# A three-layer transformer kernel in which the rounded right operands of three stages start further on within a 2,048-byte row than their weights

## The chip, the cores and the metric

The kernel runs on one core of a Trainium2 chip, on 512 positions of width 1,024. The core has five engines with queues of their own: TensorE (PE; its weight loads are shown apart, as PEld), VectorE (DVE), ScalarE (ACT), GpSimd (POOL) and SyncE (SP, which issues the transfers from memory here). They share an on-chip memory (SBUF) of 128 partitions. An address in it is a byte within a partition; a word is 4 bytes. The metric is the device time in microseconds (us) of one execution, as the median of several.

## The reference, cut to what matters

Three layers, each a mixer and a feed-forward part, run one behind the other. All their projections are products of the activations with weight matrices, in fp32:

```python
def first_block(x, ...):          # two layers: neighborhood attention, differential attention
    for i in range(DEPTH):
        h = rms_norm(x, g[0])
        m = neighborhood_attention(h, ...) if i % 2 == 0 else diff_attention(h, ...)
        x = x + rms_norm(m, g[1])
        f = conv_glu_ffn(rms_norm(x, g[2]), ffn_w_in[i], ..., ffn_w_out[i])
        ...
# third layer (the hybrid one): three mixers on one input projection, then a feed-forward part
#   p = rms(x) @ w_in                      (1024 x P_IN)
#   mix = [rwkv7(p), mla(p), gated_deltanet(p)];  x = x + mix @ w_out
#   x = x + square(relu(rms(x) @ w_ff1)) @ w_ff2     (1024 x 4096, 4096 x 1024)
```

## The kernel before

Activations lie transposed: 128 channels on the partitions, 512 positions along each. A projection's weights come from memory in chunks of 128 partitions x 1,024 words (8 blocks of 128x128), through a ring of four buffers (`ring`), asked for by SP.

Every fp32 product is made of three products of rounded numbers (type float32r). `Splitter` holds them: ACT rounds a weight chunk into `w_hi` (`round_chunk`, L278), DVE writes what was lost into `w_lo` (`split_chunk`, L284), and the right operands are split in the same way into `r_hi` and `r_lo`. `multiply` (L293 to L301) then issues for each block

```python
pe.matmul(psum, hi, self.hi(rhs_slot), start=start, stop=False)     # L299: w_hi with r_hi
pe.matmul(psum, hi, self.lo(rhs_slot), start=False, stop=False)     # L300: w_hi with r_lo
return pe.matmul(psum, lo, self.hi(rhs_slot), start=False, stop=stop)   # L301: w_lo with r_hi
```

Each of the three loads a block of 128x128 weights and streams a right operand of 128x512 words through the array. PE fetches the weights of the following product while the current one streams. The profile names operands as out<-right operand,weights.

Four kinds of stages do this. Stage `l` holds both layers of the first block (tiles `l_w_hi`, `l_r_hi`, and the further slots `na_more_hi`, `na_more_lo`, `da_more_hi`, `da_more_lo`). The hybrid layer has `in2` (`mixer_inputs`; 27 chunks, tiles `in_...` in the profile), `mt` (`mixer_tail`; 8 chunks) and `ff` (`up_down`; 32 chunks up and 32 down). Between `in2` and `mt` lie two stages without a `Splitter`. The order of the work is written out by hand: each engine runs its own list and waits on semaphores. PE waits for a chunk's split (`chunk_split`), and ACT rounds the next chunk into a slot once PE is done with the one in it (`chunk_done`).

SBUF is given out in the order in which tiles are named, one behind the other, at multiples of 32 bytes. Let the place of a tile be its address modulo 2,048 bytes (512 words), and the distance of a right operand the words by which its place lies behind that of its weights. A slot of a right operand has 512 words, and a weight chunk 1,024, so a tile behind such tiles alone has distance 0. In `l`, `in2`, `mt` and `ff`, `w_hi`, `w_lo`, `r_hi` and `r_lo` follow one another with nothing between: `r_hi` and `r_lo` have distance 0. So do `da_more_hi` and `da_more_lo`. Only `na_more_hi` and `na_more_lo` don't: three small tiles of 16 words each (`na_nmax`, `na_tot`, `na_inv`) lie ahead of them, and both have distance 48. They hold the right operands of six of the eight blocks of each chunk of the neighborhood attention's projection; the first two blocks take theirs from `l_r_hi` and `l_r_lo`. A weight block lies at a multiple of 128 words in its chunk, so these distances differ by 128, 256 or 384 words from block to block, all else equal.

Of the kernel before, what the change touches and what calls it, by code (L numbers as in the profile page):

```python
# [18 lines left out]
F32R = mybir.dt.float32r  # L19
# [7 lines left out]
P = 128  # L27
S = 512
TT = S // P
D = 1024  # L30
DT = D // P
# [26 lines left out]
SLOTS = 4  # L58
# [112 lines left out]
class Program:  # L171


    def __init__(self, nc, ctx, dram):
        self.nc, self.dram = nc, dram
        self.sb = lambda name, shape, dt=F32: ctx.enter_context(nc.sbuf_tensor(name, shape, dt))
        with ExitStack() as under:
            self.qk_hi = under.enter_context(nc.sbuf_tensor("qk_hi", [P, 4, S], F32R))
        self.X = self.sb("X", [P, DT, S])
        self.H = self.sb("H", [P, DT, S])  # L180
        self.rstd = self.sb("rstd", [P, S])
        self.ring = self.sb("ring", [P, RING, BLK * P])
        self.par = self.sb("par", [P, N_PARAMS])
        self.const = self.sb("const", [P, N_CONSTS])
        self.ring_full = [ctx.enter_context(nc.semaphore(f"ring_full{i}")) for i in range(RING)]
        self.chunk_split = ctx.enter_context(nc.semaphore("chunk_split"))
        self.const_loaded = ctx.enter_context(nc.semaphore("const_loaded"))
        self.par_loaded = ctx.enter_context(nc.semaphore("par_loaded"))
        self.x_loaded = [ctx.enter_context(nc.semaphore(f"x_loaded{j}")) for j in range(DT)]
        self.chunk_done = ctx.enter_context(nc.semaphore("chunk_done"))  # L190
        self.g = 0
# [58 lines left out]
class Splitter:  # L250
# [2 lines left out]

    def __init__(self, k, st, rhs_tiles, rhs_slots=None, slots=SLOTS):
        self.k, self.g0, self.rhs_slots, self.slots = k, k.g, rhs_slots or rhs_tiles, slots
        self.w_hi = st.sb("w_hi", [P, slots, BLK * P], F32R)
        self.w_lo = st.sb("w_lo", [P, slots, BLK * P], F32R)
        self.r_hi = st.sb("r_hi", [P, rhs_slots or rhs_tiles, S], F32R)  # L260
        self.r_lo = st.sb("r_lo", [P, rhs_slots or rhs_tiles, S], F32R)
        self.more = []
        self.w_rounded, self.rhs_rounded, self.rhs_split = (
            st.sem(n) for n in ("w_rounded", "rhs_rounded", "rhs_split"))
# [292 lines left out]
def up_down(k, name, n_up, n_down, evacuation, mid, pre):  # L557


    with Stage(k, name) as st:  # L560
        sp_ = Splitter(k, st, DT, DT + 2)
        banks = st.ps("banks", [P, 8, S])
        front = Front(k, st, sp_, None, pre, banks[:, 6:8, :])
        bank_free, tile_done, added, stored = (st.sem(n) for n in ("bank_free", "tile_done", "added", "stored"))
# [1399 lines left out]
IN_SLOTS = 3  # L1964
# [8 lines left out]
def mixer_inputs(k, pi, kr, bi, ki, pc, rows2, cols):  # L1973
# [6 lines left out]
    order = in2_order()  # L1980
    shifted = [c for c in range(IN_T) if order[c] not in (MISC, G_GATE, G_GATE + 1, G_GATE + 2, M_Q, M_Q + 1, M_KV)]
    with Stage(k, "in2") as st:
        sp_ = Splitter(k, st, DT, slots=IN_SLOTS)
        acc = st.ps("acc", [P, 4, S])
        side = st.ps("side", [P, 4, S])
        bank_a, bank_b, bank_c, bank_d = (side[:, n, :] for n in range(4))
# [1102 lines left out]
OUT_SLOTS = 3  # L3089
# [3 lines left out]
def mixer_tail(k, pi, y, la):  # L3093
# [4 lines left out]


    with Stage(k, "mt") as st:  # L3100
        sp_ = Splitter(k, st, DT, slots=OUT_SLOTS)
        a = st.ps("a", [P, 5, S])
        ms = la.ms
        vt = st.sb("vt", [P, TT, 256])
# [478 lines left out]
def hybrid(k):  # L3583

    with ExitStack() as ctx:
        def sb(name, shape):
            return ctx.enter_context(k.nc.sbuf_tensor(name, shape, F32))

        pi = sb("pi", [P, IN_T, S])
        bi = sb("bi", [P, MIX_T, S])  # L3590
        kr = sb("kr", [P, MIX_T, TT, 2, P])
        ki = sb("ki", [P, MIX_T, S])
        v, gk, gv = pi[:, R_V:R_V + MIX_T, :], pi[:, G_K:G_K + MIX_T, :], pi[:, G_V:G_V + MIX_T, :]
        y = [v[:, i, :] for i in range(MIX_T)] + [gv[:, i, :] for i in range(MIX_T)]
        with ExitStack() as ctx2:
            def sb2(name, shape):
                return ctx2.enter_context(k.nc.sbuf_tensor(name, shape, F32))

            pc, el = sb2("pc", [P, MIX_T, NCH]), sb2("el", [P, MIX_T, NCH])
            rows2 = sb2("rows2", [P, S])  # L3600
            cols = sb2("cols", [P, 120])
            mixer_inputs(k, pi, kr, bi, ki, pc, rows2, cols)
            mt, n0 = sb2("mt", [P, 2 * MIX_T, NCH, CHUNK]), sb2("n0", [P, 2 * MIX_T, NCH, CHUNK])
            rows = [pi[:, R_WA, :], pi[:, R_G, :], rows2]
            chunk_operators(k, pi, bi, kr, ki, mt, n0, pc, el, rows, cols)
            la = Latent(pi, bi, ki, kr, ctx.enter_context(k.nc.psum_tensor("la_ms", [P, 3, S], F32)))
            recurrence(k, mt, n0, [bi[:, i, :] for i in range(MIX_T)] + [gk[:, i, :] for i in range(MIX_T)], (v, gv), pi, la)
        mixer_tail(k, pi, y, la)
    with ExitStack() as ctx:
        mid = ctx.enter_context(k.nc.sbuf_tensor("mid", [P, FF2_T, S], F32))  # L3610
        up_down(k, "ff", FF2_T, FF2_T, relu_squared(k, mid), mid, "ln_ffn")
# [121 lines left out]
```

## Time and profile before

| | us |
|---|---|
| median of 3 runs | 2222.01 |
| lowest, highest | 2221.18, 2223.2 |
| span of the profiled execution | 2221.5 |

The profiled execution's span is 0.5 us under the median. The trace has 14,078 products on PE and as many weight loads. A product's time in the trace (0.39 us for one of 128x512) runs from its start to the end of its results, and the next product starts long before that end. The pace of PE is therefore read from the distance between the starts of two products that follow one another, or from the number of products in a stretch, never from a sum of their times.

### The profile page before, as it was taken

Reading aid. Unit: us, or ns where it says so; the run is one execution under the profiler, and the core shown is the slowest. Engines: PE = TensorE matmul, PEld = TensorE weight load, DVE = VectorE, ACT = ScalarE, POOL = GpSimd, SP = SyncE. Lnnn points to the kernel's source line nnn. Section 1 sums busy time; section 2 is a strip of 40 time slices with the busy share of each in tenths; the row PEclk is TensorE's granted clock in tenths of the full one; section 3 lists DMA queues with packets and bytes.
Section 4 is the critical chain, followed back from the end, with each engine's and each line's share of the span. In section 5 each row is a group of like instructions: output and inputs, shape, how many; then the busy total and the mean of one; then the engine's idle time right before and its main releaser. Section 6 shows DMA issues by size and latency. Waiting matters only on the chain. (4 is left out here: it accounts for less than half of the span.)

```text
span 2221.5 us, 35739 instructions
## 1 busy us (share of the span) xinstructions
PE 2158.3 (97%) x14078; PEld 1723.8 (78%) x14078; DVE 1289.8 (58%) x1733; ACT 907.8 (41%) x1421; POOL 119.7 (5%) x96
## 2 busy tenths in 40 slices
PE   8999999999999999999999998999898899999999
PEld 6777788888877777778888876777787566888887
DVE  5564576663378877476665347686456566333333
ACT  4444532222365666642222244654322545323321
POOL 0000011110000000001110000000333000000000
PEclk9999999999999999999999999999999999999999
DMA  7332233333324221323333331322000112333321
GB/s 255 105 107 65 76 113 96 94 98 101 94 75 134 91 66 47 105 74 106 95 100 99 94 95 50 100 85 76 3 4 4 47 39 64 107 94 102 97 94 66
DMA packets 54087, 189.77 MB, mean 85 GB/s; under 512 B 5968, under 2 KB 6224, under 8 KB 53840
## 3 DMA queue, kind: packets, MB, share of 16 engines
q1 hardware_dynamic: 53680, 187.49, 27.3%
q8 instruction: 88, 1.44, 0.3%
q10 hardware_dynamic: 288, 0.59, 0.1%
q14 instruction: 31, 0.25, 0.0%
HBM read 184.91 MB, written 3.15 MB: 85 GB/s over the span
## 5 line engine op out<-in xcount | busy, mean ns | idle before, releaser
L299 PE MATMUL l_banks<-l_r_hi,l_w_hi 128*128 128x512 f32 x1440 | 574.3, 399 | 3.5 <-DVE l_r_lo L1796 2.3
L301 PE MATMUL l_banks<-l_r_hi,l_w_lo 128*128 128x512 f32 x1440 | 561.0, 390 | 0.0
L300 PE MATMUL l_banks<-l_r_lo,l_w_hi 128*128 128x512 f32 x1440 | 560.8, 389 | 0.0
L284 DVE TENSOR_TENSOR l_w_lo<-ring,l_w_hi 128x1024 fp32r<-128x1024 f32 x216 | 299.0, 1386 | 96.0 <-ACT l_w_hi L278 92.3
L278 ACT ACTIVATE l_w_hi<-ring 128x1024 fp32r<-128x1024 f32 x216 | 227.1, 1056 | 293.8 <-PE l_banks L301 288.9
L299 PEld LDWEIGHTS l_banks<-l_r_hi,l_w_hi 128*128 128x128 f32 x1440 | 270.3, 188 | 72.7 <-issue 8.2
L300 PEld LDWEIGHTS l_banks<-l_r_lo,l_w_hi 128*128 128x128 f32 x1440 | 270.5, 188 | 57.6 <-issue 4.3
L301 PEld LDWEIGHTS l_banks<-l_r_hi,l_w_lo 128*128 128x128 f32 x1440 | 270.3, 188 | 57.0
L299 PE MATMUL ff_banks<-ff_r_hi,ff_w_hi 128*128 128x512 f32 x512 | 200.0, 391 | 0.0
L301 PE MATMUL ff_banks<-ff_r_hi,ff_w_lo 128*128 128x512 f32 x512 | 199.2, 389 | 0.0
L300 PE MATMUL ff_banks<-ff_r_lo,ff_w_hi 128*128 128x512 f32 x512 | 199.2, 389 | 0.0
L735 POOL TENSOR_TENSOR tail_mid<-H 128x512 f32 x44 | 60.0, 1365 | 1145.8 <-ACT H L728 774.0
L284 DVE TENSOR_TENSOR ff_w_lo<-ring,ff_w_hi 128x1024 fp32r<-128x1024 f32 x64 | 78.3, 1225 | 61.6 <-ACT ff_w_hi L278 58.4
L299 PEld LDWEIGHTS ff_banks<-ff_r_hi,ff_w_hi 128*128 128x128 f32 x512 | 96.1, 188 | 20.5 <-issue 0.5
L300 PEld LDWEIGHTS ff_banks<-ff_r_lo,ff_w_hi 128*128 128x128 f32 x512 | 96.1, 188 | 20.2 <-issue 0.5
L301 PEld LDWEIGHTS ff_banks<-ff_r_hi,ff_w_lo 128*128 128x128 f32 x512 | 96.1, 188 | 20.1
L292 DVE TENSOR_TENSOR l_r_lo<-tail_mid,l_r_hi 128x512 fp32r<-128x512 f32 x44 | 30.5, 692 | 130.3 <-ACT l_r_hi L288 130.3
L299 PE MATMUL in_acc<-in_r_hi,in_w_hi 128*128 128x512 f32 x216 | 90.9, 421 | 0.0
L288 ACT ACTIVATE l_r_hi<-tail_mid 128x512 fp32r (+1 forms) x44 | 27.7, 630 | 153.1 <-PE l_banks L301 153.1
L301 PE MATMUL in_acc<-in_r_hi,in_w_lo 128*128 128x512 f32 x216 | 85.0, 393 | 0.0
L300 PE MATMUL in_acc<-in_r_lo,in_w_hi 128*128 128x512 f32 x216 | 84.7, 392 | 0.0
L292 DVE TENSOR_TENSOR ff_r_lo<-mid,ff_r_hi 128x512 fp32r<-128x512 f32 x32 | 22.2, 693 | 101.6 <-ACT ff_r_hi L288 101.6
(513 smaller groups left out, 3256.9 us busy)
## 6 DMA issues: line engine op xcount, KB each, us to landing
ring<-weights SPq DMA_DIRECT2D x315, 512.0 KB, 3.6
na_bias<-window_bias SPq DMA_DIRECT2D x16, 512.0 KB, 5.4
da_rel<-t_rel SPq DMA_DIRECT2D x8, 448.0 KB, 4.2
outT<-X SPq DMA_DIRECT2D x12, 256.0 KB, 2.1
X<-xT SPq DMA_DIRECT2D x8, 256.0 KB, 5.7
const<-consts SPq DMA_DIRECT2D x1, 1312.0 KB, 11.5
l_pt<-pT SPq DMA_DIRECT2D x2, 512.0 KB, 4.6
X<-outT SPq DMA_DIRECT2D x4, 256.0 KB, 3.2
```

Source lines behind the costliest of these rows:

```text
L278: act.activation(self.w_hi[:, c % self.slots, :], k.ring[:, g % RING, :], ACT.Copy).then_inc(self.w_rounded, 1)
L284: dve.tensor_tensor(self.w_lo[:, c % self.slots, :], k.ring[:, g % RING, :], self.w_hi[:, c % self.slots, :].bitcast(F32), ALU.subtract).t ...
L288: act.activation(self.hi(slot), src, ACT.Copy).then_inc(self.rhs_rounded, 1)
L292: dve.tensor_tensor(self.lo(slot), src, self.hi(slot).bitcast(F32), ALU.subtract).then_inc(self.rhs_split, 1)
L299: pe.matmul(psum, hi, self.hi(rhs_slot), start=start, stop=False)
L300: pe.matmul(psum, hi, self.lo(rhs_slot), start=False, stop=False)
L301: return pe.matmul(psum, lo, self.hi(rhs_slot), start=False, stop=stop)
L735: pool.tensor_tensor(mid[:, f + j, :], gelu[:, j, :], value[:, j, :], ALU.mult).then_inc(mid_done, 1)
```

## The change

`Splitter` takes a pair of numbers, `apart`, and places a tile of so many words, which nothing uses, ahead of `r_hi` and another ahead of `r_lo`. The pair is (0, 0) in stage `l`, which stays as it was, (24, 8) in `in2`, (16, 24) in `mt` and (64, 200) in `ff`. The second gap adds to the first, so the distances are:

| stage | r_hi | r_lo |
|---|---|---|
| in2 | 24 | 32 |
| mt | 16 | 40 |
| ff | 64 | 264 |

No instruction is added, removed or moved on any engine; only line numbers grow by 6. The tiles allotted behind `r_lo` in the same stage (`in2_raw1` and three small ones; `mt_vt`, `mt_t2` and three small ones) move on by 32 and 40 words, and still fit.

```diff
-    def __init__(self, k, st, rhs_tiles, rhs_slots=None, slots=SLOTS):
+    def __init__(self, k, st, rhs_tiles, rhs_slots=None, slots=SLOTS, apart=(0, 0)):
...
         self.w_hi = st.sb("w_hi", [P, slots, BLK * P], F32R)
         self.w_lo = st.sb("w_lo", [P, slots, BLK * P], F32R)
-        self.r_hi = st.sb("r_hi", [P, rhs_slots or rhs_tiles, S], F32R)
-        self.r_lo = st.sb("r_lo", [P, rhs_slots or rhs_tiles, S], F32R)
+        for name, words in zip(("r_hi", "r_lo"), apart):
+            if words:
+                st.sb(f"before_{name}", [P, words])
+            tiles = st.sb(name, [P, rhs_slots or rhs_tiles, S], F32R)
+            if name == "r_hi":
+                self.r_hi = tiles
+            else:
+                self.r_lo = tiles
...
-        sp_ = Splitter(k, st, DT, DT + 2)
+        sp_ = Splitter(k, st, DT, DT + 2, apart=(64, 200))
...
-        sp_ = Splitter(k, st, DT, slots=IN_SLOTS)
+        sp_ = Splitter(k, st, DT, slots=IN_SLOTS, apart=(24, 8))
...
-        sp_ = Splitter(k, st, DT, slots=OUT_SLOTS)
+        sp_ = Splitter(k, st, DT, slots=OUT_SLOTS, apart=(16, 24))
```

## Rows read from the trace of the kernel before

**Rows 1.** The page: busy time by engine, and the chain that ended last.

```profile
PE 2158.3 (97%) x14078; PEld 1723.8 (78%) x14078; DVE 1289.8 (58%) x1733; ACT 907.8 (41%) x1421; POOL 119.7 (5%) x96
PE 15%; DVE 1%; ACT 0%; issue 0%; DVEq 0%
```

**Rows 2.** Windows: each engine's busy time and count in stages in2, mt, ff.

```profile
core 0: us, PE busy (x) PEld busy (x) DVE busy (x) ACT busy (x) POOL busy (x), PEclk, DMA share, GB/s
1389.00:1562.00 173.00, 172.14 (x727) 133.20 (x725) 119.85 (x162) 93.80 (x129) 0.00 (x0) 0.99 0.28 83
1790.00:1864.00 74.00, 70.37 (x382) 48.93 (x381) 43.63 (x68) 24.82 (x56) 0.00 (x0) 1.00 0.15 43
1880.00:2213.00 333.00, 333.00 (x1470) 275.53 (x1469) 117.85 (x125) 98.58 (x126) 0.00 (x0) 1.00 0.30 90
```

**Rows 3.** Waits of PE in the window of ff, then of in2.

```profile
PE ff_banks L402 <- DVE H L390: 0.8, 1, 0.8
...
PE in_side L2028 <- ACT bi L2104: 0.5, 2, 0.3
```

**Rows 4.** Groups by line, operands and shape in in2, mt and ff.

```profile
L299 PE MATMUL in_acc<-in_r_hi,in_w_hi 128*128 128x512 f32 x216 | 90.9, 421 | 0.0
L299 PE MATMUL mt_a<-mt_r_hi,mt_w_hi 128*128 128x512 f32 x34 | 14.6, 429 | 0.0
L299 PE MATMUL la_ms<-mt_r_hi,mt_w_hi 128*128 128x512 f32 x30 | 12.6, 419 | 0.0
L299 PE MATMUL ff_banks<-ff_r_hi,ff_w_hi 128*128 128x512 f32 x512 | 200.0, 391 | 0.0
```

**Rows 5.** Timeline of ff: products and weight loads (start us, us, what).

```profile
1885.15 0.39 PE L299 MATMUL ff_banks<-ff_r_hi,ff_w_hi 128*128 128x512 f32 x1
1885.15 0.19 PEld L300 LDWEIGHTS ff_banks<-ff_r_lo,ff_w_hi 128*128 128x128 f32 x1
1885.37 0.39 PE L300 MATMUL ff_banks<-ff_r_lo,ff_w_hi 128*128 128x512 f32 x1
```

**Rows 6.** Timeline of PE in in2, 18 products apart.

```profile
1491.20 0.39 PE L299 MATMUL in_acc<-in_r_hi,in_w_hi 128*128 128x512 f32 x1
...
1495.28 0.39 PE L299 MATMUL in_acc<-in_r_hi,in_w_hi 128*128 128x512 f32 x1
```

**Rows 7.** Timeline of PE in the first attention, 14 products apart, distance 48.

```profile
100.59 0.39 PE L299 MATMUL l_banks<-na_more_hi,l_w_hi 128*128 128x512 f32 x1
...
103.86 0.40 PE L301 MATMUL l_banks<-na_more_hi,l_w_lo 128*128 128x512 f32 x1
```

**Rows 8.** Timeline of the weight loads of unrounded fp32 products, ff's start.

```profile
1864.48 0.19 PEld L333 LDWEIGHTS ff_banks<-const 128*128 128x128 f32 x1 [0.24 <-issue]
...
1866.63 0.19 PEld L333 LDWEIGHTS ff_banks<-const 128*128 128x128 f32 x1 [0.24 <-issue]
```

**Rows 9.** Timeline of PE in in2 around an interrupting product.

```profile
1455.96 1.02 PE L2034 MATMUL in_side<-H,const 128*128 128x512 f32 x2
1456.41 0.79 PE L299 MATMUL in_acc<-in_r_hi,in_w_hi 128*128 128x512 f32 x1
1457.05 0.39 PE L300 MATMUL in_acc<-in_r_lo,in_w_hi 128*128 128x512 f32 x1
...
1458.20 0.40 PE L299 MATMUL in_acc<-in_r_hi,in_w_hi 128*128 128x512 f32 x1
```

**Rows 10.** The writer of the rounded operands at distance 48 and 0.

```profile
L1057 ACT ACTIVATE na_more_hi<-X,par x6: 707/718/726, 9.1 to 12.3; 128x512 fp32r<-128x512 f32 x6
L1057 ACT ACTIVATE l_r_hi<-X,par x2: 706/706/707, 7.9 to 8.5; 128x512 fp32r<-128x512 f32 x2
```

**Rows 11.** Groups in ff: who feeds PE there.

```profile
L284 DVE TENSOR_TENSOR ff_w_lo<-ring,ff_w_hi 128x1024 fp32r<-128x1024 f32 x61 | 74.7, 1225 | 59.4 <-ACT ff_w_hi L278 56.2
L292 DVE TENSOR_TENSOR ff_r_lo<-mid,ff_r_hi 128x512 fp32r<-128x512 f32 x32 | 22.2, 693 | 101.6 <-ACT ff_r_hi L288 101.6
```

## The prediction

> **What bounds the kernel now.** I read the page's engine shares first, then the busy times of windows cut at the stages, then PE's waits in those windows, and last single starts in the timeline. PE is busy for 97% of the span, and the chain that ended last is nearly all PE where it could be followed [rows 1]. In ff PE is busy for all 333 us of the window, in in2 for 172.1 of 173, in mt for 70.4 of 74 [rows 2], and the longest waits for another engine are 0.8 us in ff and 0.5 us in in2 [rows 3]. DVE has 118 us of work in ff's 333 and ACT 99. So the time of these stages is the number of PE's products times the distance between their starts, and what changes that distance changes the time one for one.
>
> The distance follows from rows. In ff, 1470 products fall into 333 us; two of them are half-products of a sum over ones. That leaves 333 / 1468 = 0.2268 us each [rows 2]. In in2, two starts 18 products apart are 1495.28 - 1491.20 = 4.08 us apart, or 0.2267 [rows 6]. The places of the operands in memory differ between the two stages (1,920 bytes into the row in ff, 544 in in2), and the pace doesn't. In the first attention, where the right operand has distance 48, two starts 14 products apart are 103.86 - 100.59 = 3.27 us apart, or 0.2336 [rows 7]. So equal places give 0.2267 wherever they are, and a distance of 48 words gives 0.2336: it is the relative place that matters, if it is place at all, and it is worth 6.9 ns a product.
>
> What could tie the two: the load of the next weights starts within 10 ns of the product's start and lasts 0.19 us of its 0.227 us [rows 5]. Two reads of the same memory run side by side, one through 128 words and one through 512. 512 columns at the granted 2.4 GHz (clock 1.00 in ff [rows 2]) are 213.3 ns, so 13.4 ns of each product are something else at distance 0, and 20.3 ns at distance 48. Both are close to whole steps of 6.67 ns, 16 cycles: two steps and three. For a product that streams slower the surcharge is gone: an unrounded fp32 half-product of 512 columns takes (1866.63 - 1864.48) / 5 = 0.430 us [rows 8], which is 1,024 cycles (426.7 ns) and 3 ns.
>
> **The change part by part.** It adds no instruction, no transfer and no wait. Three things move.
>
> First, the right operands of 3 x 216 products in in2, 3 x (34 + 30) in mt and 3 x 512 in ff [rows 4]: 648 + 192 + 1536 = 2376 products, of 14,078. Their unknown is the new distance between starts. Bounds from rows: below, half of the unrounded half-product, 215 ns, 11.8 ns under today [rows 8]; above, 233.6 at distance 48 [rows 7], 6.8 ns over today. On all 2376 products these are -28 and +16 us.
>
> I take one step less than today, 220.0 ns, which is the nearest pace in steps of 6.67 ns on the lower side, 6.8 ns under ff's average. The reasons are these. Where both reads begin at the same place and at the same time, they ask for the same part of the row together; a distance can separate them. The three stages' distances are all other than the one known to be bad, and r_lo has another distance than r_hi, which neither of the two known cases has. Against it stands the only other distance that the trace shows, which is slower.
>
> - ff: 1536 x 6.8 ns = 10.4 us.
> - in2: the pace of 0.2267 is reached only after some products. Behind an interrupting product the starts are (1458.20 - 1457.05) / 5 = 0.230 us apart [rows 9], and it takes about ten products to come down. There are 727 products in in2's window [rows 2], 648 of them of this kind, in runs that some fifteen small groups interrupt; that leaves about 500 at the settled pace. 500 x 6.7 ns = 3.3 us.
> - mt: 192 such products among 382 [rows 2], interrupted everywhere; perhaps 60 are settled: 0.4 us.
>
> Second, the writers of these tiles, ACT and DVE, write to new places. An activation into a tile at distance 48 takes 718 ns in the median against 706 at distance 0 [rows 10]; 12 ns on the 32 splits of a right operand in ff's second half [rows 11] would be 0.4 us of DVE or ACT time, under PE, which has 5.4 us per chunk (24 x 0.2267) against DVE's 1.23 + 0.69 us. Cost: nothing. Were that cover gone it would be 0.4 us in ff and less elsewhere.
>
> Third, mt_vt, mt_t2, in2_raw1 and the small tiles move by 40 or 32 words. Vector and scalar work reads them under PE's cover, and mt_vt serves 80 short products whose pace nothing here ties to place. Nothing, with 0.5 us either way.
>
> If PE gets faster, can the feed follow? A chunk would take 24 x 0.220 = 5.28 us. Weights come at 90 GB/s with DMA busy for 0.30 of the time [rows 2], and DVE's work for a chunk is 1.9 us. Nothing becomes late.
>
> Sum: 10.4 + 3.3 + 0.4 = 14.1 us less. The profiled execution's span is 2221.5 us, so 2207.4; the median of the runs is 0.5 us over the span, so 2207.9. I say 2208.
>
> **Two rules of the Trainium skill.** The trace shows 0.2267 us at distance 0 and 0.2336 at distance 48 [rows 6, 7]. The page "TensorE: Matmul & The Clock Gate", section "Step-by-step: what each phase is for", says that PE has two independent SBUF read ports and that loading the next weights doesn't steal read bandwidth from the running product. By it the change does nothing and the time stays 2222, a rival below; the 6.9 ns between the two rows speak against it. The same page's section "Wait — 56ns, not 53.3ns?" gives the columns divided by 2.4 GHz and 2.5 ns as the distance of back-to-back products. For 512 columns this would be 215.8 ns, 11 ns under the rows here; if the change brought all 2376 products to it, the estimate would be 2196 us. No product of this kind in the rows shows that pace.
>
> **Rivals.**
>
> 1. *Slower: the settled pace needs equal places.* For: the one distance other than 0 that the trace shows costs a step more [rows 7], and a run that is out of step, as behind an interruption, goes at 0.230 even at distance 0 [rows 9]. Against: one distance is no law, and at 48 the two right operands have the same distance. Price: with a step more on the same products, 1536 x 6.8 + 500 x 6.9 + 60 x 6.9 ns = 10.4 + 3.5 + 0.4 = 14.3 us, so 2236. It decides in ff: as soon as ff's starts are more than 226.8 ns apart, the kernel is slower, since in2 and mt have together less than half of ff's settled products.
> 2. *No change: place doesn't matter, or these distances fall on the same parts of the memory as 0.* For: in ff r_hi has a distance of 64 words, and if the pattern repeats every 64 words or less, two of three products there see what they see today; a weight block's place changes by 128 words from one to the next without effect, as the even pace in ff shows [rows 2]. Then what is slow at distance 48 would be the neighbours of that stage, DVE and ACT on the same memory. Against: in in2 DVE and ACT are as busy (120 and 94 of 173 us) and the settled pace is 0.2267 [rows 2, 6]. Time: 2222.
> 3. *The whole surcharge goes.* All 2376 products at 215 ns: 28 us less, 2194. For: the slower stream has none [rows 8]. Against: nothing shows it for rounded operands. I count it within the forecast's side, with a small part of its chance.
>
> **How the numbers follow.** The forecast (one step less, or near it) has 0.47, the whole surcharge gone 0.10, slower 0.28, no change 0.15. A change within 0.2% (4.4 us) cannot be told from none. A mixed outcome, where ff gains and the others lose or the other way, lies within the same span; small ones (a gain of a step on one product in three, 5 us) I put with faster. Faster is then 0.58, same 0.15, slower 0.27. The likeliest case alone would be 2201 to 2216. The range reaches down to where the whole surcharge goes, 2194, and up to just under the price of rival 1: 2194 to 2235 leaves out about 2 in 10.
>
> **What the profile after would show.** In ff, a window of 333 us would hold 1513 products at 220 ns, 1468 if nothing changed, and 1427 at 233.4. The same reading in in2's quiet stretches, and the length of in2 and mt. The first attention and all of stage l must stay as they are. The weight loads should still start with the product and last 0.19 us. If ff is faster and its starts aren't at a step of 6.67 ns, the step is wrong though the direction is right. If DVE or ACT appears among PE's waits in ff, the feed is the new bound. If ff's starts are 233 ns apart, rival 1 holds and I am wrong in sign.

## The result and the profile after

The changed kernel is slower: 2236.61 us in the median (2235.24 to 2236.85, 4 runs) against 2222.52 us (2221.18 to 2223.2, 4 runs), a ratio of 1.0056 with a 95% interval of 1.0044 to 1.0068. The profiled execution has a span of 2234.8 us, 13.3 us over before's. I had forecast 2208, within a range of 2194 to 2235, and had given slower a chance of 0.27.

The first view is the one that answers to [rows 2]: busy time and count of each engine in windows of the changed kernel.

```profile
core 0: us, PE busy (x) PEld busy (x) DVE busy (x) ACT busy (x) POOL busy (x), PEclk, DMA share, GB/s
1389.00:1562.00 173.00, 172.36 (x715) 130.86 (x714) 119.92 (x162) 93.82 (x130) 0.00 (x0) 0.99 0.27 83
1790.00:1864.00 74.00, 72.30 (x381) 48.76 (x380) 45.15 (x70) 26.28 (x57) 0.00 (x0) 1.00 0.14 43
1884.00:2217.00 333.00, 333.00 (x1429) 268.61 (x1428) 116.66 (x123) 97.90 (x125) 0.00 (x0) 1.00 0.30 90
```

The reader should look at the counts. In ff, 333 us hold 1429 products where they held 1470; less the two that reach in over the edges, that is 333 / 1427 = 0.2334 us each. In in2, 173 us hold 715 where they held 727. The clock is the same (1.00, 0.99), PE is as full as before and no wait of PE for another engine stands in ff's window. The chain that ended last is made of the same lines as in [rows 1], with 6 added to their numbers.

The second view, the timeline of PE in in2 of the changed kernel, answers to [rows 6]; again 18 products lie between the starts.

```profile
1492.11 0.40 PE L305 MATMUL in_acc<-in_r_hi,in_w_hi 128*128 128x512 f32 x1
...
1496.32 0.40 PE L305 MATMUL in_acc<-in_r_hi,in_w_hi 128*128 128x512 f32 x1
```

4.21 / 18 = 0.2339 us, against 0.2267. The third is the timeline of PE in ff, answering to [rows 5].

```profile
1899.89 0.40 PE L305 MATMUL ff_banks<-ff_r_hi,ff_w_hi 128*128 128x512 f32 x1
1900.12 0.40 PE L306 MATMUL ff_banks<-ff_r_lo,ff_w_hi 128*128 128x512 f32 x1
1900.12 0.19 PEld L307 LDWEIGHTS ff_banks<-ff_r_hi,ff_w_lo 128*128 128x128 f32 x1
1900.35 0.39 PE L307 MATMUL ff_banks<-ff_r_hi,ff_w_lo 128*128 128x512 f32 x1
```

The weight load still starts with the product and lasts 0.19 us. Only the distance between the products' starts has grown. The trace holds the starts in whole nanoseconds, and all means below are worked out from these. The distances repeat as 232, 232, 236 in the first half of ff and as 233, 236, 231 in the second: 700 ns for three, where before it was 226, 227, 227, or 680.

Where the 13.3 us went: in in2, the two windows that hold the same work, 732 products each, are 178 us long before and 181 us after. First the row of the kernel before, then that of the changed one.

```profile
1384.00:1562.00 178.00, 176.90 (x732) 135.39 (x732) 123.71 (x168) 98.58 (x136) 0.00 (x0) 0.98 0.28 82
```

```profile
1384.00:1565.00 181.00, 180.04 (x732) 135.08 (x732) 123.69 (x168) 98.52 (x136) 0.00 (x0) 0.98 0.27 81
```

That is 3.0 us, but in2's first product starts 0.25 us earlier in the changed kernel. From the start of the first to that of the last of its 648 products it is 171.9 us before and 175.3 after: 3.3 us. ff gives (233.28 - 226.73) ns x 1536 = 10.0 us, with the mean distances of its directly following products; from its first product to its last it is 9.9, since the pause between its two halves is 0.2 us shorter. mt has 0.3 us, and what lies outside the three stages is 0.2 us shorter. The first attention stands as before, at 233.3 ns in both kernels.

ACT and DVE do their work in the same time as before: 93.4 and 134.2 us in ff in both kernels, 58.4 and 77.5 in in2, 40.4 and 47.8 in mt, each counted over the instructions on that stage's tiles.

### The profile page after: what moved, and what is told of

It reads as the page before. It is cut to its first block and busy times, and to the rows that moved or that the text cites. A ratio compares the mean times of both kernels' runs of the same rounds, so it can differ in the third digit from the quotient of the medians.

```text
span 2234.8 us, 35739 instructions
## 1 busy us (share of the span) xinstructions
PE 2173.1 (97%) x14078; PEld 1725.8 (77%) x14078; DVE 1289.8 (58%) x1733; ACT 907.7 (41%) x1421; POOL 119.6 (5%) x96
## 5 line engine op out<-in xcount | busy, mean ns | idle before, releaser
L305 PE MATMUL l_banks<-l_r_hi,l_w_hi 128*128 128x512 f32 x1440 | 574.8, 399 | 3.9 <-DVE l_r_lo L1802 2.3
L307 PE MATMUL l_banks<-l_r_hi,l_w_lo 128*128 128x512 f32 x1440 | 561.5, 390 | 0.0
L306 PE MATMUL l_banks<-l_r_lo,l_w_hi 128*128 128x512 f32 x1440 | 561.2, 390 | 0.0
L284 ACT ACTIVATE l_w_hi<-ring 128x1024 fp32r<-128x1024 f32 x216 | 227.1, 1056 | 293.8 <-PE l_banks L307 288.8
L305 PEld LDWEIGHTS l_banks<-l_r_hi,l_w_hi 128*128 128x128 f32 x1440 | 270.6, 188 | 73.0 <-issue 8.3
L306 PEld LDWEIGHTS l_banks<-l_r_lo,l_w_hi 128*128 128x128 f32 x1440 | 270.8, 188 | 57.9 <-issue 4.3
L307 PEld LDWEIGHTS l_banks<-l_r_hi,l_w_lo 128*128 128x128 f32 x1440 | 270.5, 188 | 57.1
L306 PE MATMUL ff_banks<-ff_r_lo,ff_w_hi 128*128 128x512 f32 x512 | 204.7, 400 | 0.0
L305 PE MATMUL ff_banks<-ff_r_hi,ff_w_hi 128*128 128x512 f32 x512 | 203.0, 397 | 0.0
L307 PE MATMUL ff_banks<-ff_r_hi,ff_w_lo 128*128 128x512 f32 x512 | 201.2, 393 | 0.0
L305 PEld LDWEIGHTS ff_banks<-ff_r_hi,ff_w_hi 128*128 128x128 f32 x512 | 96.7, 189 | 25.2 <-issue 0.5
L307 PEld LDWEIGHTS ff_banks<-ff_r_hi,ff_w_lo 128*128 128x128 f32 x512 | 96.2, 188 | 22.9
L306 PEld LDWEIGHTS ff_banks<-ff_r_lo,ff_w_hi 128*128 128x128 f32 x512 | 96.1, 188 | 21.9 <-issue 0.5
L305 PE MATMUL in_acc<-in_r_hi,in_w_hi 128*128 128x512 f32 x216 | 92.1, 427 | 0.0
L307 PE MATMUL in_acc<-in_r_hi,in_w_lo 128*128 128x512 f32 x216 | 86.1, 399 | 0.0
L306 PE MATMUL in_acc<-in_r_lo,in_w_hi 128*128 128x512 f32 x216 | 85.6, 396 | 0.0
```

The source lines that it names most:

```text
L284: act.activation(self.w_hi[:, c % self.slots, :], k.ring[:, g % RING, :], ACT.Copy).then_inc(self.w_rounded, 1)
```

## The experiments

Whole kernels are compared with runs of the kernel before on the same chip in the same rounds: 5 runs of ff alone and 11 or 12 of each of the others, against 15 to 21 of the kernel before. The kernels of products alone ran once each, for their trace.

**ff alone.** The change with in2 and mt left as they were:

```diff
-        sp_ = Splitter(k, st, DT, slots=IN_SLOTS, apart=(24, 8))
+        sp_ = Splitter(k, st, DT, slots=IN_SLOTS)
...
-        sp_ = Splitter(k, st, DT, slots=OUT_SLOTS, apart=(16, 24))
+        sp_ = Splitter(k, st, DT, slots=OUT_SLOTS)
```

> The gaps of the changed kernel in stage ff alone: distances 64 and 264 there, 0 in in2 and mt. Theory A (a product settles at 226.7 ns only where right operand and weights have the same place, and at 233.3 otherwise): ff loses (233.3 - 226.7) ns x 1536 = 10.2 us, in2 and mt stand as before; 2232.5. Theory B (the loss came from in2 and mt, whose products are interrupted, ff's is small): within 3 us of before. Theory C (the times of the stages hang on what was before them): not the sum of parts; anything else.

Measured: 2231.41 us against 2223.74, a ratio of 1.0035 (1.0021 to 1.0049), so 7.7 us. Its window in ff:

```profile
1884.00:2217.00 333.00, 333.00 (x1440) 269.75 (x1439) 116.49 (x123) 95.58 (x122) 0.00 (x0) 1.00 0.30 88
```

333 / 1438 = 0.2316 us, not 0.2333. Most of the loss is ff's, against theory B. The size, 7.7 us where theory A has 10.2, could be noise by the times alone (the interval is 4.7 to 10.9 us), but the trace shows that the same places give another pace here: twelve starts that repeat (230 233 226 226 236 233 233 234 230 236 229 234 ns, 231.7 in the mean).

**in2 and mt alone.** The changed kernel with ff back at distance 0:

```diff
-        sp_ = Splitter(k, st, DT, DT + 2, apart=(64, 200))
+        sp_ = Splitter(k, st, DT, DT + 2)
```

> The changed kernel's gaps in in2 and mt alone, ff at distance 0. With ff alone the loss was 7.7 us, in both parts together 14.1. Theory P (parts add up): 14.1 - 7.7 = 6.4 us slower, 2228.6. Theory Q (ff has two rhythms at distances 64 and 264, 231.7 ns when entered as in the kernel with ff alone and 233.3 as in the changed kernel, 2.6 us apart): in2 loses about 500 x 6.7 ns = 3.3 us and mt under 1, so 3.5 to 4.5 us slower, 2226.5, and ff's starts are 226.7 ns apart.

Measured: 2226.76 us against 2222.94, a ratio of 1.0017 (1.0008 to 1.0026), so 3.8 us. The parts, 7.7 and 3.8, make 11.5 of 14.1 us. The intervals of the three times are too wide (1.8 to 5.8 us for this one) to show by themselves that 2.6 us are missing. The traces speak for theory Q: ff's mean distance is 233.28 ns in the changed kernel and 231.66 with ff alone, which on 1536 products is 2.5 us. Each of the two has one trace, so that a kernel always settles at the same pace isn't shown. Its window in ff is back at before's pace, 333 / 1469 = 0.2267 us:

```profile
1884.00:2217.00 333.00, 333.00 (x1471) 275.72 (x1470) 118.44 (x126) 97.91 (x126) 0.00 (x0) 1.00 0.30 90
```

**A whole row in ff.** As ff alone, but the gap is 512 words:

```diff
-        sp_ = Splitter(k, st, DT, DT + 2, apart=(64, 200))
+        sp_ = Splitter(k, st, DT, DT + 2, apart=(512, 0))
```

> A gap of 512 words, a whole row of 2,048 bytes, ahead of r_hi in ff, none ahead of r_lo; in2 and mt as before. Everything in ff lies elsewhere, but at distance 0 within the row. Theory A: no change, 2222.5, and ff's starts 226.7 ns apart. Theory D (what costs is that operands don't follow one another directly, or where they lie in the whole memory, not in the row): slower by up to 10 us like the changed kernel.

Measured: 2223.25 us against 2223.74, a ratio of 0.9998 (0.9989 to 1.0007). A gap costs nothing by itself, nor does another address in the same place of a row; theory D falls, and theory A holds.

**8 words fewer in ff.** As ff alone, with 192 words instead of 200 ahead of r_lo:

```diff
-        sp_ = Splitter(k, st, DT, DT + 2, apart=(64, 200))
+        sp_ = Splitter(k, st, DT, DT + 2, apart=(64, 192))
```

> Stage ff with gaps of 64 and 192 words, 8 fewer than the changed kernel ahead of r_lo: distances 64 and 256. in2 and mt at 0. Theory A64 (the pattern repeats every 64 words, as the sweep shows with nothing else running): both count as 0, starts 226.7 ns apart, the time of before, 2223. Theory A512 (the place in the whole row counts, since in a stage with DVE and ACT at work more of the address matters): slower, 2231 to 2234.

Measured: 2222.64 us against 2222.21, a ratio of 1.0001 (0.9992 to 1.001). Its window in ff:

```profile
1884.00:2212.00 328.00, 328.00 (x1449) 271.60 (x1448) 115.86 (x123) 95.64 (x122) 0.00 (x0) 1.00 0.30 90
```

Less the two at the edges, 328 / 1447 = 0.2267 us: theory A64 holds. Distances 64 and 256 count as 0, in the full kernel too. So of ff's change only 8 words were at work: those by which 264 passes 256, in r_lo, the operand of one product in three.

**The one uneven place made even.** The kernel before, with the first attention's further slots moved from distance 48 to 0:

```diff
+            na_sb("before_more", [P, 464])
             more_slots(na_sb)
```

> The kernel before with 464 unused words ahead of na_more_hi, so that the first attention's further slots have distance 0 where they had 48. Theory A: their 432 products settle at 226.7 ns instead of 233.5, 432 x 6.8 = 2.9 us less where PE is the bound; 2219.6. Theory E (they were slow because of what DVE and ACT do beside them, not because of the distance): no change, and the starts stay 233 ns apart.

Measured: 2221.29 us against 2223.74, a ratio of 0.9989 (0.998 to 0.9998): 2.4 us less, against 2.9 expected, and only just clear of noise. Its timeline answers to [rows 7], once more 14 products apart:

```profile
99.69 0.39 PE L299 MATMUL l_banks<-na_more_hi,l_w_hi 128*128 128x512 f32 x1
...
102.87 0.39 PE L301 MATMUL l_banks<-na_more_hi,l_w_lo 128*128 128x512 f32 x1
```

3.18 / 14 = 0.2271 us instead of 0.2336; over all its directly following products the mean goes from 233.3 to 227.1. DVE and ACT do beside it what they did, so theory E falls. This version beats the kernel before; the gain is as small as the stretch.

**Products alone, by place.** A kernel of its own, that leaves the three layers out: groups of 72 products in threes as in `multiply`, with no other engine at work. Its core (a and b number the tiles that serve as r_hi and r_lo):

```diff
+PLACES = [8 * n for n in range(64)]
+PAIRS = [(n, n) for n in range(64)] + [(0, n) for n in range(64)] + [(n, 0) for n in range(64)]
...
+                for n, (a, b) in enumerate(PAIRS):
+                    pe.matmul(banks[:, 4 + n % 4, :], X[:, 0, 0:P], X[:, 5, :], start=True, stop=True)
+                    for t in range(REPEAT):
+                        cols = slice(t % 8 * P, t % 8 * P + P)
+                        mm = triple(pe, banks[:, n % 4, :], w_hi[:, cols], w_lo[:, cols], tiles[a][:, :], tiles[b][:, :],
+                                    t == 0, t == REPEAT - 1)
```

> A kernel of its own that leaves the three layers out and times the products alone: 192 groups of 72 products (24 blocks, three each, as in multiply), with nothing else running. First 64 groups: both right operands at distance 0, 8, 16, ... 504. Next 64: r_hi at 0 and r_lo at these. Last 64: r_hi at these and r_lo at 0. Theory A: 226.7 ns at distance 0 alone (or at 0 and at multiples of some shorter period such as 128), 233.3 elsewhere; then no place beats equal places. Theory F (the steps go further down): some distances settle at 220 ns or less. Theory E (the other engines cause the difference): all distances alike.

Measured, as the mean of each group's last 24 distances between starts, in ns:

| words | 0 | 8 | 16 | 24 | 32 | 40 | 48 | 56 |
|---|---|---|---|---|---|---|---|---|
| both | 226.7 | 233.3 | 228.9 | 233.3 | 232.7 | 234.4 | 233.3 | 233.3 |
| r_lo only | 226.7 | 231.7 | 231.8 | 231.1 | 233.3 | 231.1 | 228.9 | 231.1 |
| r_hi only | 226.7 | 231.1 | 233.3 | 232.2 | 228.9 | 232.3 | 234.5 | 233.3 |

From 64 words on everything repeats, to within 0.1 ns, eight times over the row. Two groups in the timeline, each with 36 products between its rows: distance 64, then 72.

```profile
196.66 0.39 PE L17 MATMUL banks<-t_at,w_lo 128*128 128x512 f32 x1
204.82 0.39 PE L17 MATMUL banks<-t_at,w_lo 128*128 128x512 f32 x1
...
214.08 0.39 PE L17 MATMUL banks<-t_at,w_lo 128*128 128x512 f32 x1
222.48 0.39 PE L17 MATMUL banks<-t_at,w_lo 128*128 128x512 f32 x1
```

8.16 / 36 = 0.2267 and 8.40 / 36 = 0.2333 us. With nothing else running, 0 gives 226.7, 48 gives 233.3, and 0 with 8 gives 231.7: what before's ff, the first attention and ff alone show. So the cause lies in PE and the places of its operands. Theory A holds, with a period of 64 words; theories E and F fall.

**All pairs of places.** 64 pairs of r_hi and r_lo and eight groups in which w_lo moves with r_lo, 144 products each:

```diff
+GROUPS = [(8 * a, 8 * b, 0, 128) for a in range(8) for b in range(8)] + [(0, 8 * b, 8 * b, 128) for b in range(8)]
...
+                        mm = triple(pe, banks[0:cols, n % 4, :], w_hi[:, at:at + cols], w_lo[:, l + at:l + at + cols],
+                                    r_hi[:, a:a + S], r_lo[:, b:b + S], t == 0, t == REPEAT - 1)
```

> Products alone, the layers left out: 64 groups of 144 products, every pair of distances of r_hi and r_lo from 0, 8, ... 56, then 8 groups with r_hi at 0 and r_lo and w_lo both at 0, 8, ... 56. If only the right operand and the weights loaded beside it matter, taken pair by pair, the last 8 groups settle at 226.7 ns (r_lo streams while w_lo is loaded, at the same place). If what matters is how one right operand lies to the one before it, they are as slow as r_lo alone at that distance: 231.7, 231.8, 231.1, 233.3, 231.1, 228.9, 231.1 in the sweep. Of the 64: theory A says that none is below 226.7; theory F, that some pair off the axes is.

Measured over the last 60 distances: only the pair (0, 0) settles at 226.7. Seven pairs settle at 228.9, all others between 230.4 and 235.6. in2's pair (24, 32) gives 233.3, as in the changed kernel, and mt's (16, 40) 230.4 (in the kernels, where mt's products are often interrupted, their mean goes from 229.9 to 231.5). The pair (0, 32) settles at 231.1 here, but at 233.3 in the sweep above and in the one below: two rhythms at the same places, with nothing but PE at work. With w_lo moved along with r_lo the pace is 232.2, 231.1, 228.9, 231.1, 231.8, 233.3 and 231.7: so r_lo at the place of the weights that load beside it is not enough. The pairwise theory falls; nor do these groups equal r_lo alone. Windows over the group in which all four are at 0, then over that with r_lo and w_lo at 8:

```profile
2212.00:2240.00 28.00, 28.00 (x125) 23.19 (x124) 0.00 (x0) 0.00 (x0) 1.00 0.00 1
2245.00:2273.00 28.00, 28.00 (x122) 22.65 (x121) 0.00 (x0) 0.00 (x0) 1.00 0.00 1
```

The same 28 us hold three products fewer, as means of 226.7 and 232.2 ns make it.

**Word by word.** The same kernel with these groups:

```diff
+GROUPS = [(n, n, 0, 128) for n in range(64)] + [(0, n, 0, 128) for n in range(64)] + [(n, 0, 0, 128) for n in range(64)]
```

> Products alone: 192 groups of 72, in steps of one word from 0 to 63: both right operands, r_lo alone, r_hi alone. If lines of 4 words (16 bytes) are read, distances of 0 to 3 differ from one another, since an unaligned operand touches one line more, and 4 behaves like a place between 0 and 8. If lines of 8 words or more are read, it is 8 that counts. Theory A: no distance is faster than 0. Theory F: a distance that is no multiple of 8 settles at 220 ns or less.

Measured: single words matter. With both operands moved, 226.7 ns comes back at 7, 15, 28, 39, 47, 59 and 63 words, and 240.0 stands at 5, 25, 33, 49, 57 and 61. Lines of 4 words are borne out in part: distances of 0 to 3 differ (226.7, 236.7, 233.3, 228.9), 4 lies between 0 and 8 (231.7), and over the row the 16 distances that are 3 over a multiple of 4 have a mean of 229.0, those that are 1 over one of 237.6. But the multiples of 4 differ among themselves as much, from 226.7 to 236.7. Nothing in 192 groups settles below 226.7, so theory F falls again. Five words, then seven, 36 products between the rows:

```profile
115.78 0.40 PE L17 MATMUL banks<-r_hi,w_lo 128*128 128x512 f32 x1
124.42 0.40 PE L17 MATMUL banks<-r_hi,w_lo 128*128 128x512 f32 x1
...
151.12 0.39 PE L17 MATMUL banks<-r_hi,w_lo 128*128 128x512 f32 x1
159.28 0.39 PE L17 MATMUL banks<-r_hi,w_lo 128*128 128x512 f32 x1
```

8.64 / 36 = 0.2400 and 8.16 / 36 = 0.2267 us.

**Narrower weights.** The same kernel with 128, 96, 64 and 32 columns of weights:

```diff
+GROUPS = [(8 * d, 8 * d, 0, cols) for cols in (128, 96, 64, 32) for d in range(8)]
```

> Products alone, weights of 128, 96, 64 and 32 columns, each with both right operands at 0, 8, ... 56; 144 products a group. If the surcharge over 213.3 ns is the weight load in the way of the stream, it shrinks with the columns: 13.3 ns at 128, about 10, 6.7 and 3.3 at distance 0, and 20 falls to 5 at the slow distances. If it is a fixed cost of a product, it stays at 13.3 and 20.

Measured: no shrinking. At 96 columns distance 8 settles at 226.7 (where 128 columns give 233.3) and distance 0 at 230.0; at 32 columns the groups lie between 230.6 and 240.0. A load lasts 189 ns in the mean at 128 columns and 108 at 32, so the surcharge isn't the length of the weight load, nor is it fixed. Nor is an equal place the best one here: at 96 columns it is distance 8, and at 64 columns distance 40 (226.7, against 230.0 at 0). Distance 8 at 96 columns, then 56 at 32, 60 products between the rows:

```profile
344.82 0.39 PE L17 MATMUL banks<-r_hi,w_lo 128*96 128x512 f32 x1
358.42 0.40 PE L17 MATMUL banks<-r_hi,w_lo 128*96 128x512 f32 x1
...
1095.41 0.41 PE L17 MATMUL banks<-r_hi,w_lo 128*32 128x512 f32 x1
1109.81 0.39 PE L17 MATMUL banks<-r_hi,w_lo 128*32 128x512 f32 x1
```

**Lengths, one kind alone, and bf16.**

```diff
+GROUPS = ([('three', d, n) for n in (512, 384, 256, 128) for d in (0, 8, 16, 48)] + [('one', d, 512) for d in (0, 8, 16, 48)]
+          + [('bf16', d, 512) for d in (0, 8, 16, 48)])
```

> Products alone, the layers left out. Right operands of 512, 384, 256 and 128 columns at distances 0, 8, 16 and 48 (144 products a group, three kinds in turn as in multiply); then one kind of product repeated (w_hi with r_hi) at these distances; then the same with operands in bf16. If the surcharge belongs to each product whatever its length, starts are 13.3 ns over columns / 2.4 GHz at distance 0 for all lengths, and about 20 at 8 and 48. If the stream pays by the column, it is 10, 6.7 and 3.3 ns for the shorter ones. If the turn from r_hi to r_lo and back matters, one kind repeated is as fast at every distance. If it belongs to the type float32r, bf16 shows 213.3 to 216 ns at every distance.

Measured over the last 60 distances, in ns, at distances 0, 8, 16, 48; in brackets what columns / 2.4 GHz make:

| | 0 | 8 | 16 | 48 |
|---|---|---|---|---|
| 512 columns, three kinds (213.3) | 226.7 | 233.3 | 228.9 | 233.3 |
| 384 (160.0) | 173.3 | 173.3 | 173.3 | 173.3 |
| 256 (106.7) | 120.0 | 116.7 | 117.8 | 113.3 |
| 128 (53.3) | 111.7 | 111.6 | 111.7 | 111.7 |
| 512, one kind | 226.7 | 233.3 | 228.9 | 233.3 |

One kind repeated has the same four values, so the turn between r_hi and r_lo isn't needed. At 384 and 128 columns the four places give the same pace, and at 256 the order turns round: distance 48 is the fastest, 0 the slowest. 256 columns at distance 0, then at 48, 60 products between the rows:

```profile
271.91 0.28 PE L19 MATMUL banks<-r_hi,w_lo 128*128 128x256 f32 x1
279.11 0.28 PE L19 MATMUL banks<-r_hi,w_lo 128*128 128x256 f32 x1
...
324.99 0.28 PE L19 MATMUL banks<-r_hi,w_lo 128*128 128x256 f32 x1
331.79 0.28 PE L19 MATMUL banks<-r_hi,w_lo 128*128 128x256 f32 x1
```

7.20 / 60 = 0.1200 and 6.80 / 60 = 0.1133 us. In bf16 the distances between starts are 215 to 217 ns at all four places, with a mean of 215.8 at each. Windows over the bf16 groups at distance 0 and 48:

```profile
538.00:567.00 29.00, 28.89 (x134) 13.12 (x134) 0.00 (x0) 0.00 (x0) 1.00 0.00 1
634.00:663.00 29.00, 28.84 (x133) 13.14 (x135) 0.00 (x0) 0.00 (x0) 1.00 0.00 1
```

134 and 135 weight loads in 29 us (a few products have no record there): about 0.216 us each.

## Why the prediction was wrong

**The bound** was right: these stages are the number of PE's products times the distance between their starts, and the feed never became late. (The 0.5 us that it calls in2's longest wait is the total of two; the longest is 0.3 [rows 3].) So was the reading that the relative place is what matters, by distance 0 in two stages and 48 in a third; the run with a whole row's gap and the one with the first attention's place made even confirm it. The counts were right: 1536, and about 500 settled ones in in2, where 469 of the 605 directly following distances are 226 or 227 ns. So was costing the writers and the moved tiles at nothing, as the equal times of ACT and DVE in the three stages show. The 12 ns that a write at distance 48 seemed to cost aren't the place's either: with the first attention's slots moved to distance 0 the same writes still take 718 ns in the median.

**The step that failed** is the pace at the new places: "I take one step less than today, 220.0 ns, which is the nearest pace in steps of 6.67 ns on the lower side". The changed kernel settled one step higher, at 233.3, in ff and in2. The reason that I gave, that "a distance can separate them", took distance 0 for the worst place, where two reads ask for the same part together. The sweeps show the reverse: of 64 pairs of places in steps of 8 words, 0 with 0 is the fastest and the only one at 226.7, and no pace under it came up in steps of one word either. With that, ff's 10.4 us, in2's 3.3 and mt's 0.4 had the wrong sign: they measured 9.9, 3.3 and 0.3 us of loss. The row I had for an uneven place [rows 7] was slower, and it was the only evidence on the sign; I argued it away by saying that there both operands have the same distance. Moving both, r_lo alone or r_hi alone costs 2 to 8 ns in all cases of the table.

The steps of 6.67 ns failed too, as a rule: 226.7, 233.3 and 240.0 lie on them, but 228.9, 230.4 and ff alone's 231.7 don't. And the 0.2336 read over 14 products [rows 7] is 233.3 over all of the first attention's, so a step was worth 6.6 ns and not 6.9.

**Rival 1** (the settled pace needs equal places) was the right one: 2236 forecast, 2236.61 measured. Its terms were 10.4 us in ff, 3.5 in in2 and 0.4 in mt; measured were 9.9, 3.3 and 0.3. Three details were off. A place need not be equal in the row, only modulo 64 words in steps of 8, and in steps of one word seven other distances reach 226.7 as well. Rival 2 was right that r_hi's 64 counts as 0, and wrong that two of three products then see what they saw: r_lo's 8 words slow down all three (235.9, 231.3 and 232.6 ns behind L306, L307 and L305, against 226.4, 227.0 and 226.8 before). And "a step more" isn't the only outcome: with ff alone changed, the same places settled at 231.7, at a loss of 7.7 us in place of 10. That the time came out to within a microsecond is partly luck: nothing in the prediction told which of the two rhythms ff would take, and the traces have 13.3 us between them where rival 1 had 14.3.

**The two rules weighed.** In bf16 512 columns took 215.8 ns at the four places tried, and in float32r at best 226.7. The Trainium skill's "TensorE: Matmul & The Clock Gate", section "Wait — 56ns, not 53.3ns?", adds about 2.5 ns to the columns over 2.4 GHz, an estimate of 215.8 ns: the bf16 groups agree, the float32r ones don't. The rule in section "Step-by-step: what each phase is for" of that page, that loading weights takes no read bandwidth from the running product, agrees with the bf16 groups, whose pace doesn't know the place. For float32r it did not help: by it alone the place would make no difference, and with 512 columns and weights of 128 it made up to 13.3 ns.

**The unrounded half-product** [rows 8] was a bad lower bound: at half the pace it has only 3 ns over its columns, but no placing brought a float32r product of 512 columns near half of that.

**What stays open** is the mechanism under the rhythm. Shown are: it lies in PE and the places of its operands; it showed with float32r at 512 columns, turned round at 256, and didn't show at 384, at 128 or in bf16 at the four places tried; it repeats every 64 words in steps of 8; and a settled rhythm repeats, after 3 products in the changed ff and after 12 in ff alone. That the product's read and the next weights' read meet in the memory would fit the rule of places, but isn't shown: narrower weights didn't lower the cost, and putting w_lo and r_lo at one place didn't restore 226.7. Why ff takes one rhythm or another at the same places is open: in the changed kernel and in ff alone the code and places of ff are the same, and what comes before it isn't. The pair (0, 32) had two rhythms without any other stage or engine at work, so neither is needed for it. Unrounded fp32 products were tried at no other place.

## What to carry to other kernels

Where TensorE is the bound, read the distance between the starts of products, not their durations, and compare it between stages that do the same work: 226.7 against 233.3 ns in one trace was the whole effect, with its sign. For float32r products of 512 columns with weights of 128 columns keep right operands and weights at equal addresses modulo 256 bytes; small tiles allotted between them break this unseen (48 words did here, for 2.4 us). With narrower weights or 256 columns measure first: there another place was faster. An argument on why a memory place should be better needs a measured case on its side: the single uneven place in the trace was worth more than the picture of two reads in each other's way.

## What the runs showed of the hardware that was not expected

- A stream of float32r products settles into a rhythm whose mean depends on the relative places of its operands: 226.7 to 240.0 ns for 512 columns at a granted clock of 1.00, repeating every 64 words in steps of 8. The lowest is 13.3 ns over 512 / 2.4 GHz. In bf16 it is 215.8 ns at the four places tried.
- The same places can have two rhythms: 231.7 and 233.3 ns in ff at 64 and 264 words, 2.5 us of the kernel apart, and 231.1 and 233.3 ns for the pair (0, 32) with products alone.
- With weights of 96 or 64 columns an equal place is no longer the best: 230.0 ns there, 226.7 at distance 8 and 40.
- For 256 columns the best and worst places change sides: 113.3 ns at distance 48 and 120.0 at 0.
- For 128 columns the pace is 111.7 ns at the four places tried, twice what the columns need (53.3).
